# Summing modulation rows on VectorE and GpSimd before TensorE adds the partitions

## The chip, the cores and the metric

One core of one Trainium2 chip runs the whole program. The metric is device time in microseconds (us), the median over runs. Engines: TensorE (PE, with its weight loads as PEld), VectorE (DVE), ScalarE (ACT), GpSimd (POOL) and SyncE (SP), which only issues DMAs. All data are fp32.

## The reference, cut to what matters

Two transformer blocks run one after the other on 512 tokens of 1024 features. Each is steered by a modulation, a vector times a matrix:

```
mod   = silu(c)     @ w_ada    + b_ada       # block 1: (1, 3072): shift, scale, gate
mod   = silu(c_2)   @ w_ada_2  + b_ada_2     # block 2: (1, 6144): shift, scale, gate, shift2, scale2, gate2
mod_c = silu(c_ctx) @ w_ada_2  + b_ada_2     # block 2, for the context rows
```

Block 1: norm and modulate, projections of 3072 columns, a recurrent branch (convolution, gates, a scan) and a dilated attention, output projection, gated sum. Block 2: norm and modulate, projections, pooling, differential attention, an RWKV branch, gates, a merge and a mixture of 32 experts with two per token. The modulation is 9216 columns of a matrix with 1024 rows: 18 chunks of 512 columns. Chunks 0 to 3 (shift and scale of block 1) are needed at once; the change concerns chunks 4 to 17. Chunks 4 and 5 serve one vector (c), 6 to 9 two (c_2 and c_ctx), 10 to 17 only c_2.

## The kernel before, in words

The program is written by hand, engine by engine. Each stage has a function for each engine (`proj1_tensor`, `proj1_vector`, ...), and five program functions at the end call them in order; each engine runs its list in that order and waits on semaphores. VectorE, ScalarE and GpSimd also wait for their own last instruction before the next (`Line`, lines 90 to 210). All instructions of one kind therefore have one line in the profile (154 two tensors, 159 and 160 with scalars, 164 scalar and tensor, 168 copy, 172 reciprocal, 176 fill, 192 scan, 204 activation, 207 matmul, 210 transpose, 143 DMA).

Weights lie in DRAM as chunks of 128x4096, 2 MB each. SyncE streams them into three buffers in the order of `MAIN_CHUNKS` (line 323); a load waits until TensorE has used the chunk three places earlier (`load`). A chunk of the modulation holds its 1024 rows as 8 groups k of 128 partitions, with 512 columns each.

The stages up to the change's last step, in order:

- Preparation: modulation chunks 0 to 3, first norm.
- First projections (`proj1_*`): 24 steps t (chunks 6 to 11 of the stream, four tiles each) of 8 matmuls 128x128 by 512. The recurrent branch runs beside them (`lru_*`): VectorE convolves at steps 0 to 3, ScalarE and VectorE make its gates, VectorE scans at steps 4 to 7, ScalarE squares at step 8; at step 9 TensorE sums the squares. At steps 8 to 15 VectorE copies each tile (`raw1`) and TensorE turns it by a matmul one step later (`rotate`).
- Attention of block 1 (`att_*`): 35 steps x for 32 pairs of query block (128 to 512 keys) and head. In a step TensorE does the scores of x+1, transposes x-2 and multiplies x-3 with the values; VectorE adds a mask and takes the maximum; ScalarE does the exponential and copies the transposes. Four times, once per query block, ScalarE leaves for a square and a square root, with a table load on both sides.
- Output projection (`out1_*`): four row tiles of two matmul groups, then norms of six row tiles on VectorE and ScalarE (`normed`), each turned by TensorE (`turn8`).
- Projections of block 2 (`proj2_*`).

Modulation chunks 4 to 17 go through TensorE. `modulation_blocks` multiplies each 128x128 block of a chunk by the vectors, held as 32 columns of which three count; the 32 rows of result for each quarter t of the chunk go to partitions 32t to 32t+31, so one bank's 128 columns hold all 512:

```
for k in ks:
    for t in range(4):
        T.mm(b[32 * t:32 * t + 32, 0:128], cs[:, k, :], w[:, k, c4(t)], k == 0, k == 7)
```

A chunk is 32 such matmuls, and an fp32 matmul leaves two records in the trace. Chunks 4 to 15 are dealt out in thirds (`ADA`, `ADA_K`, line 863), one third to an attention step (`ada_tensor`); chunks 16 and 17 follow the output projection in `out1_tensor`. `ada_vector` adds the bias (kept as 128 partitions in the arena), `ada_gpsimd` stores the rows to `mods1` and `mods2` in DRAM, from where they are read back, broadcast to 128 partitions. GpSimd otherwise only issues DMAs and fills buffers in these stages.

## Time and profile before

| | us |
|---|---|
| median of 3 runs (lowest, highest) | 1869.82 (1866.83, 1871.75) |
| the profiled execution: span, which is the only time given for it | 1876.8 |
| TensorE busy in it | 1717.6 |
| VectorE, ScalarE, GpSimd busy | 804.7, 518.8, 109.4 |
| first projections, from the first matmul to the first scores | 36.9 to 221.9 |
| attention of block 1 | 221.9 to 309.6 |
| output projection, to the last quarter of the first tile of block 2 | 309.6 to 391.4 |

A row of the profile gives a line of the program, an engine, an operation, what it writes and reads (`arena` is the one SBUF tensor, `psum` the accumulators, `in_w` the chunks in DRAM), how often, the busy time, the mean duration, and the idle time in front of it with what ended it. TensorE's records overlap, so that busy times of groups of its rows can sum to more than the stretch. PEclk is the granted clock as a share of 2.4 GHz.

### The profile page before, as it was taken

How to read it: one execution, taken by the hardware profiler on the slowest of the kernel's cores; microseconds unless marked ns; L12 is line 12 of the kernel's file. 1: busy time of each engine (PE TensorE's matmuls, PEld its weight loads, DVE VectorE, ACT ScalarE, POOL GpSimd, SP SyncE). 2: the span in 40 equal slices, each digit the busy share in tenths (PEclk: the TensorE clock that was granted, in tenths of full speed). 3: DMA queues.
4: the chain of work that ended last, by engine and by line, in shares of the span. 5: the costliest groups of instructions: out<-in, count | busy, mean ns of one | idle time of the engine just before them, and what ended most of it. 6: DMA issues, size and time to landing. Idle time of an engine off the chain costs nothing.

```text
span 1876.8 us, 37887 instructions
## 1 busy us (share of the span) xinstructions
PE 1717.6 (92%) x16822; PEld 927.4 (49%) x16822; DVE 804.7 (43%) x1484; ACT 518.8 (28%) x983; POOL 109.4 (6%) x144
## 2 busy tenths in 40 slices
PE   5999999999999999999999999999999977778786
PEld 3444566544546555556667667544454333323332
DVE  3853144656627456355654554344462211222210
ACT  3710254311127422354453341122231110101010
POOL 0000010010000000100000000000001101010100
PEclk8999989999989999999998998899999999999998
DMA  9121376351110030042221210356569999999997
GB/s 396 76 88 47 145 287 247 145 224 69 45 45 1 23 151 0 17 170 82 77 81 50 63 56 24 114 219 221 219 239 398 416 425 415 422 413 425 417 423 279
DMA packets 48360, 359.25 MB, mean 191 GB/s; under 512 B 8325, under 2 KB 8557, under 8 KB 28736
## 3 DMA queue, kind: packets, MB, share of 16 engines
q1 hardware_dynamic: 35792, 311.51, 41.2%
q0 software_dynamic: 12400, 45.27, 7.3%
q8 instruction: 134, 2.20, 0.5%
q14 instruction: 34, 0.28, 0.0%
HBM read 337.47 MB, written 27.32 MB: 194 GB/s over the span
## 4 chain that ended last, share of the span: by engine, by line
PE 74%; DMA 16%; ACT 4%; issue 3%; DVE 2%; POOL 0%; SPq 0%; ACTq 0%; DVEq 0%; POOLq 0%
PE psum L207 71%; DMA arena<-in_w 16%; PE psum L210 3%; ACT arena L204 3%; ACT L204 1%; DVE arena L154 1%; DVE arena L180 0%; DVE arena L164 0%; DVE arena L172 0%; DVE arena L160 0%; POOL arena L141 0%; DMA arena<-in_tok 0%; DVE arena L168 0%; DVE arena L159 0%; POOL out L149 0%
## 5 line engine op out<-in xcount | busy, mean ns | idle before, releaser
L207 PE MATMUL psum<-arena 32*32 32x16 f32 (+12 forms) x16178 | 1638.1, 304 | 145.2 <-DMA arena<-in_w 73.4
L207 PEld LDWEIGHTS psum<-arena 32*32 32x32 f32 (+5 forms) x16178 | 856.0, 135 | 876.3 <-issue 764.7
L204 ACT ACTIVATE arena<-psum 128x512 f32<-128x512 f32 (+5 forms) x334 | 171.4, 513 | 871.2 <-PE psum L207 670.7
L154 DVE TENSOR_TENSOR arena<-arena,psum 128x512 f32<-128x512 f32 (+3 forms) x128 | 64.9, 507 | 402.6 <-PE psum L207 209.2
L154 DVE TENSOR_TENSOR arena<-arena 128x512 f32<-128x512 f32 (+10 forms) x315 | 191.6, 608 | 31.0 <-ACT arena L204 14.7
L204 ACT ACTIVATE arena<-arena 128x512 f32<-128x512 f32 (+10 forms) x254 | 138.8, 546 | 177.7 <-DVE arena L154 41.9
L204 ACT ACTIVATE arena<-psum,arena 128x128 f32<-128x128 f32 (+3 forms) x221 | 111.7, 505 | 275.1 <-PE psum L210 135.5
L154 DVE TENSOR_TENSOR arena<-psum,arena 128x128 f32<-128x128 f32 (+3 forms) x116 | 47.4, 409 | 154.5 <-PE psum L207 141.3
L164 DVE SCALAR_TENSOR_TENSOR arena<-arena 128x512 f32<-128x512 f32 (+7 forms) x162 | 103.5, 639 | 14.5 <-ACT arena L204 8.1
L210 PE MATMUL psum<-arena 128*128 128x128 f32 x644 | 102.6, 291 | 6.1 <-ACT arena L204 3.2
L172 DVE RECIPROCAL arena<-arena 128x1 f32<-128x1 f32 (+4 forms) x71 | 79.1, 1113 | 63.0 <-ACT arena L204 59.2
L210 PEld LDWEIGHTS psum<-arena 128*128 128x128 f32 x644 | 73.6, 146 | 64.3 <-issue 46.0
L164 DVE SCALAR_TENSOR_TENSOR arena<-psum,arena 128x512 f32<-128x512 f32 (+4 forms) x84 | 49.6, 591 | 114.8 <-PE psum L207 111.2
L204 ACT ACT_TABLE_LOAD x68 | 87.2, 1283 | 18.8 <-DMA arena<-gd 11.6
L159 DVE TENSOR_SCALAR arena<-arena 128x32 f32<-128x32 f32 (+10 forms) x126 | 39.8, 316 | 57.7 <-ACT arena L204 52.7
L184 DVE COPY_PREDICATED arena<-arena,psum 128x512 f32<-128x512 uint32 (+1 forms) x60 | 35.9, 598 | 45.4 <-PE psum L207 41.3
L168 DVE COPY arena<-psum 128x512 f32<-128x512 f32 (+4 forms) x53 | 27.8, 525 | 63.2 <-PE psum L210 35.4
L180 DVE TENSOR_REDUCE arena<-psum 128x1 f32<-128x768 f32 x32 | 30.6, 958 | 47.8 <-PE psum L207 46.0
L149 POOL DMA_INDIRECT out<-arena x16 | 25.1, 1566 | 408.6 <-DVE arena L164 139.5
L143 POOL DMA_DIRECT2D arena<-kd x28 | 21.1, 753 | 240.9 <-DVE arena L154 135.3
L143 POOL DMA_DIRECT2D mods<-arena x26 | 14.4, 557 | 312.4 <-DVE arena L154 304.2
L160 DVE TENSOR_SCALAR arena<-psum,arena 128x128 f32<-128x128 f32 x64 | 26.2, 410 | 8.5 <-PE psum L210 5.0
(49 smaller groups left out, 177.7 us busy)
## 6 DMA issues: line engine op xcount, KB each, us to landing
arena<-in_w SPq DMA_DIRECT2D x127, 2048.0 KB, 34.5
arena<-in_w SPq DMA_DIRECT2D x48, 256.0 KB, 3.1
arena<-in_w SPq DMA_DIRECT2D x12, 1024.0 KB, 36.4
arena<-kd POOLq DMA_DIRECT2D x28, 256.0 KB, 3.4
gd<-arena SPq DMA_DIRECT2D x24, 256.0 KB, 3.2
arena<-gd SPq DMA_DIRECT2D x24, 256.0 KB, 5.6
arena<-in_w POOLq DMA_DIRECT2D x2, 2048.0 KB, 9.6
kd<-arena POOLq DMA_DIRECT2D x2, 1536.0 KB, 11.0
```

What stands on the lines that cost most here:

```text
L143: self.e.dma_start(out, in_).then_inc(*signal)
L154: return self.ends(self.e.tensor_tensor(out, a, b, op))
L159: return self.ends(self.e.tensor_scalar(out, a, s1, None, op0))
L160: return self.ends(self.e.tensor_scalar(out, a, s1, s2, op0, op1))
L164: return self.ends(self.e.scalar_tensor_tensor(out=out, in0=a, scalar=s, in1=b, op0=op0, op1=op1))
L168: return self.ends(self.e.tensor_copy(out, a))
L172: return self.ends(self.e.reciprocal(out, a))
L180: return self.ends(self.e.tensor_reduce(out, a, AX, op, negate=negate))
L184: return self.ends(self.e.copy_predicated(out, mask, a))
L204: return self.ends(self.e.activation(out, a, func, **kw))
L207: return self.ends(self.e.matmul(out, lhs, rhs, start=start, stop=stop))
L210: return self.ends(self.e.transpose(out, a, ident))
```

## The change

VectorE and GpSimd now do the multiplication by the vector: for each chunk and vector, eight blocks of 128x512 are scaled by a per-partition number and summed, which leaves 128 partitions to add. TensorE does that with a column of ones (`one_column`): four matmuls for each sum. VectorE sums chunks 4 to 7 between the steps of the first projections (`ADA_ROWS`), from half chunks that SyncE loads into two buffers of their own; GpSimd sums chunks 8 to 17 from quarter chunks that it loads itself into two more, one multiplication and one addition per block, from the first projections on, with four buffers for its sums. The bias now goes into DRAM first and the rows are added to it by an accumulating DMA. These chunks leave the stream of weights; `ADA_SUMS` says at which step TensorE adds, `STORES` behind which quarter GpSimd stores. The diff, cut to its core:

```diff
+    def add(self, out, in_, signal):
+        self.e.dma_start(out, in_, accum_op=ALU.add).then_inc(*signal)
...
-YTBANK = (2,)
+YTBANK = (4,)
...
-MAIN_CHUNKS = [0, 1, 2, 3, 6, 7, 8, 9, 10, 11, 4, 5, *range(14, 24), 12, 13, 24, 25, *range(26, 34), *range(40, 45)]
+MAIN_CHUNKS = [0, 1, 2, 3, 6, 7, 8, 9, 10, 11, 12, 13, *range(26, 34), *range(40, 45)]
...
+            V.zero(cs[:, 0, 16:17], value=1.0)
...
         def proj1_sync():
-            for c in (6, 7, 8, 9, 10, 11):
+            for c in (6, 7, 8):
                 load(c)
+            half_load(0)
+            half_load(1)
+            load(9)
+            load(10)
+            half_load(2)
+            half_load(3)
+            load(11)
+            for n in (4, 5, 6, 7):
+                half_load(n)
...
                 lru_tensor(t)
+                if ("p1", t) in ADA_SUMS:
+                    ada_tensor(ADA_SUMS["p1", t], ALL8)
...
                 lru_vector(t)
+                if ("p1", t - 1) in ADA_SUMS:
+                    ada_vector(ADA_SUMS["p1", t - 1])
+                for n in range(*ADA_ROWS.get(t, (0,))):
+                    ada_rows_vector(n)
...
+        ADA = (4, 8, 5, 6, 9, 7, 10, 11, 12, 13, 14, 15, 16, 17)
+        BY_VECTOR = (4, 5, 6, 7)
+        ADA_VECTORS = {j: (0,) if j < 6 else (1, 2) if j < 10 else (1,) for j in ADA}
+        ADA_SUMS = {("p1", 11): 4, ("p1", 13): 8, ("p1", 16): 5, ("p1", 19): 6, ("p1", 20): 9, ("p1", 21): 7, ("p1", 22): 10,
+                    ("att", 0): 11, ("att", 4): 12, ("att", 18): 13, ("att", 30): 14, ("out1", 1): 15, ("out1", 3): 16, ("pool", 2): 17}
+        ADA_ROWS = {7: (0, 2), 8: (2, 4), 9: (4, 8), 10: (8, 10), 13: (10, 13), 14: (13, 16), 15: (16, 18), 16: (18, 21),
+                    17: (21, 24), 18: (24, 28), 19: (28, 32)}
+        BY_POOL = [(j, v) for j in range(8, 18) for v in ADA_VECTORS[j]]
...
+        def ada_rows_vector(n):
+
+            j, k = 4 + n // 8, n % 8
+            w = half_in[n // 4 % 2][:, k % 4, :]
+            if k % 4 == 0:
+                V.wait_ge(d_ah[n // 4 % 2]["half", n // 4])
+            for v in ADA_VECTORS[j]:
...
+                    V.ts(ada_sum(j, v), w, cs[:, k, v:v + 1], None, ALU.mult)
+                else:
+                    V.stt(ada_sum(j, v), w, cs[:, k, v:v + 1], ada_sum(j, v), ALU.mult, ALU.add)
...
+        def ada_rows_gpsimd(n):
+
+            j, q = 8 + n // 4, n % 4
+            G.wait_ge(d_ap[n % 2]["piece", n])
+            for v in ADA_VECTORS[j][::-1]:
+                s = BY_POOL.index((j, v))
+                if q == 0 and s > 3:
+                    G.wait_ge(T["ada", BY_POOL[s - 4][0]])
+                for k in range(2):
+                    w, by = piece_in[n % 2][:, k, :], cs[:, 2 * q + k, v:v + 1]
+                    if q == 0 and k == 0:
+                        G.ts(sums_g[s % 4], w, by, None, ALU.mult)
+                    else:
+                        t = w if v == 1 else sqj
+                        G.ts(t, w, by, None, ALU.mult)
+                        G.tt(sums_g[s % 4], sums_g[s % 4], t, ALU.add)
+            G.then_inc("piece", n)
...
+        def ada_tensor(j, ring):
+            T.wait_ge(V["half", 2 * j - 7] if j in BY_VECTOR else G["piece", 4 * j - 29], *ps.take(ring, "ada", j))
+            last = ADA_VECTORS[j][-1]
+            for v in ADA_VECTORS[j]:
+                for t in range(4):
+                    T.mm(ps["ada", j][32 * t:32 * t + 32, 0:128], one_column(v), ada_sum(j, v)[:, c4(t)],
+                         v == ADA_VECTORS[j][0], v == last)
+            T.then_inc("ada", j)
...
         def lru_gpsimd():
...
+            STORES = {9: (4,), 10: (8,), 14: (5,), 17: (6,), 18: (9,), 20: (7,), 22: (10,), 23: (11,), 25: (12,), 29: (13,), 33: (14,), 37: (15,)}
+            piece_load(0)
+            piece_load(1)
+            for n in range(40):
+                ada_rows_gpsimd(n)
+                if n + 2 < 40:
+                    piece_load(n + 2)
+                for j in STORES.get(n, ()):
+                    ada_gpsimd(j)
...
-                ada_tensor(*next(steps), MBANK)
+                if ("att", x) in ADA_SUMS:
+                    ada_tensor(ADA_SUMS["att", x], MBANK)
...
-            for step in steps:
-                ada_tensor(*step, MBANK)
...
-            for j in (16, 17):
-                for q in range(3):
-                    ada_tensor(j, q, ALL8)
```

## Rows read from the trace of the kernel before

**Rows 1.** The page, part 1: busy time, share of the span, instructions.
```profile
PE 1717.6 (92%) x16822; PEld 927.4 (49%) x16822; DVE 804.7 (43%) x1484; ACT 518.8 (28%) x983; POOL 109.4 (6%) x144
```

**Rows 2.** The page, part 4: the chain of waits by engine.
```profile
PE 74%; DMA 16%; ACT 4%; issue 3%; DVE 2%; POOL 0%; SPq 0%; ACTq 0%; DVEq 0%; POOLq 0%
```

**Rows 3.** Busy time by stretch: PE, PEld, DVE, ACT, POOL, clock, DMA share, GB/s.
```profile
57.00:106.50 49.50, 49.50 (x117) 22.00 (x116) 42.24 (x45) 32.87 (x38) 0.00 (x0) 1.00 0.20 69
...
168.00:221.90 53.90, 53.90 (x128) 23.59 (x126) 4.47 (x7) 5.46 (x8) 0.00 (x0) 1.00 0.18 70
221.90:309.60 87.70, 86.23 (x1009) 56.83 (x1009) 44.85 (x95) 46.99 (x112) 11.06 (x20) 0.94 0.74 280
```

**Rows 4.** Weight loads grouped by shape, attention (221 to 310 us): busy, mean ns, idle.
```profile
L207 PEld LDWEIGHTS psum<-arena 128*32 128x32 f32 x724 | 18.5, 113 | 6.1 <-issue 4.8
```

**Rows 5.** Timeline, attention: start, length, instruction, idle before it.
```profile
243.87 0.59 PEld L207 LDWEIGHTS psum<-arena 128*32 128x32 f32 x24 [0.17 <-issue]
244.66 0.88 PEld L207 LDWEIGHTS psum<-arena 128*128 128x128 f32 x6 [0.20 <-issue]
...
250.38 2.35 PE L207 MATMUL psum<-arena 128*128 128x64 f32 x6 [1.11 <-ACT arena L204]
```

**Rows 6.** Busy time by stretch of 2 us, attention; the clock is third from last.
```profile
250.00:252.00 2.00, 1.62 (x6) 1.09 (x6) 0.50 (x2) 1.72 (x5) 1.01 (x2) 0.69 0.93 213
252.00:254.00 2.00, 2.00 (x20) 0.96 (x22) 1.11 (x2) 0.63 (x4) 0.00 (x0) 0.50 0.99 426
```

**Rows 7.** VectorE's instructions grouped by shape, 57.0 to 106.6 us.
```profile
L164 DVE SCALAR_TENSOR_TENSOR arena<-arena 128x512 f32<-128x512 f32 x13 | 9.5, 733 | 0.5
L154 DVE TENSOR_TENSOR arena<-arena 128x512 f32<-128x512 f32 x12 | 8.3, 692 | 0.4
L192 DVE TENSOR_TENSOR_SCAN arena<-arena 128x512 f32<-128x512 f32 x4 | 4.9, 1224 | 0.1
...
L159 DVE TENSOR_SCALAR arena<-arena 128x512 f32<-128x512 f32 x4 | 1.7, 426 | 0.1
L160 DVE TENSOR_SCALAR arena<-arena 128x512 f32<-128x512 f32 x3 | 1.6, 547 | 3.7 <-ACT arena L204 3.6
```

**Rows 8.** Timeline of VectorE, first projections (steps 8, 9 and 20).
```profile
108.69 0.69 DVE L168 COPY arena<-psum 128x512 f32<-128x512 f32 x1 [2.20 <-PE psum L207]
...
116.41 0.69 DVE L154 TENSOR_TENSOR arena<-psum,arena 128x512 f32<-128x512 f32 x1 [6.31 <-PE psum L207]
...
202.01 0.69 DVE L154 TENSOR_TENSOR arena<-arena,psum 128x512 f32<-128x512 f32 x1 [26.68 <-ACT arena L204]
```

**Rows 9.** GpSimd's instructions grouped by shape, the whole span.
```profile
L143 POOL DMA_DIRECT2D mods<-arena x26 | 14.4, 557 | 312.4 <-DVE arena L154 304.2 <-DVE arena L172 8.2
L176 POOL MEMSET arena<- 128x1024 f32 x8 | 7.6, 952 | 130.1 <-ACT arena L204 129.7
...
L176 POOL MEMSET arena<- 128x256 f32 x2 | 0.6, 311 | 0.1
```

**Rows 10.** DMA issues: count, KB each, us to landing (issued at 37.1 us).
```profile
arena<-in_norm_att POOLq DMA_DIRECT2D x1, 256.0 KB, 12.9
```

**Rows 11.** Timeline, 784 to 800 us: GpSimd's fills and a scan of VectorE.
```profile
787.76 9.09 POOL L176 MEMSET arena<- 128x1024 f32 x12 [129.71 <-ACT arena L204]
...
790.85 1.23 DVE L192 TENSOR_TENSOR_SCAN arena<-arena 128x512 f32<-128x512 f32 x1
```

**Rows 12.** Timeline, end of the output projection.
```profile
373.75 3.70 PE L207 MATMUL psum<-arena 128*32 128x128 f32 x128
...
381.20 8.44 PE L207 MATMUL psum<-arena 128*128 128x384 f32 x16 [3.75 <-DMA arena<-in_w]
...
382.63 1.23 DVE L154 TENSOR_TENSOR arena<-arena 128x1024 f32<-128x1024 f32 x1
...
389.48 1.04 PE L210 MATMUL psum<-arena 128*128 128x128 f32 x8
```

**Rows 13.** Busy time by stretch of 10 us, output projection; the clock is third from last.
```profile
380.00:390.00 10.00, 8.80 (x21) 5.10 (x22) 3.26 (x5) 1.04 (x3) 3.06 (x5) 0.66 0.95 394
```

More of the change, by code:

```diff
@@ L414, in build @@
             dma(n) for n in ("par", "cst", "x", "bias", "lnc", "pos", "wbd", "na")]
-        d_mod = [dma(f"mod{i}") for i in range(3)]
+        d_mod = [dma(f"mod{i}") for i in range(5)]
         d_g1, d_n1, d_n3, d_tb, d_xd, d_br, d_rw, d_gn = [
@@ L450, in build @@
         XA, XC = ar.get(2064, m=4, s=516), ar.get(2048, m=4, s=512)
+        half_in = [r0[:, 2048 * i:2048 * i + 2048].rearrange("p (k n) -> p k n", k=4) for i in range(2)]
+        sums_v = [bsum[:, 512 * i:512 * i + 512] for i in range(3)] + [sq1[:, 512 * i:512 * i + 512] for i in range(2)]
+        piece_in = [A_[:, NCOL - 4096 + 1024 * i:NCOL - 3072 + 1024 * i].rearrange("p (k n) -> p k n", k=2) for i in range(2)]
+        sums_g = [A_[:, NCOL - 2048 + 512 * i:NCOL - 1536 + 512 * i] for i in range(4)]
         dead = Arena(A_, 0, ar.top)
@@ L463, in build @@
         Sb, Pb, PTb, YB = [*sl[0:2], Sb3], [sl[2], sl[3], Pb3], sl[4:6], sl[6:8]
+        arow = [ar.get(128) for _ in range(5)]
         YBT = XA.rearrange("p m s -> p (m s)")[:, 0:2048].rearrange("p (m s) -> p m s", m=4)
@@ new lines, in piece_load @@
+        def piece_load(n):
+            if n > 1:
+                G.wait_ge(G["piece", n - 2])
+            G.dma(piece_in[n % 2].rearrange("p k n -> p (k n)"), T_["w"][ada_chunk(8 + n // 4), :, 1024 * (n % 4):1024 * (n % 4) + 1024],
+                  d_ap[n % 2].up("piece", n))
+        def ada_rows_gpsimd(n):
[9 more added lines that the diff above has]
+                        G.ts(sums_g[s % 4], w, by, None, ALU.mult)
+                    else:
+                        t = w if v == 1 else sqj
+                        G.ts(t, w, by, None, ALU.mult)
+                        G.tt(sums_g[s % 4], sums_g[s % 4], t, ALU.add)
+            G.then_inc("piece", n)
@@ L882, in ada_vector @@
             ps.free(V.last(), "ada", j)
         def ada_gpsimd(j):
-            G.wait_ge(V["ada", j])
-            for v in ((0,) if j < 6 else (1, 2)):
+            p = ADA.index(j)
+            G.wait_ge(V["ada", j], d_bias["mods2"])
+            for v in ADA_VECTORS[j]:
                 dst = mods1[j * 512:(j + 1) * 512] if j < 6 else mods2[v - 1, (j - 6) * 512:(j - 5) * 512]
-                G.dma(dst.rearrange("(t n) -> t n", t=4), mrow[j % 3][v:128:32, :], d_mod[j % 3].up("mod", j))
+                G.add(dst.rearrange("(t n) -> t n", t=4), arow[p % 5][v:128:32, :], d_mod[p % 5].up("mod", j))
@@ L890, in mods_stored @@
         def mods_stored(j):
-            return [d_mod[i % 3]["mod", i] for i in range(max(4, j - 2), j + 1)]
-        def lru_sync():
-            for j in range(4, 16):
-                load(ada_chunk(j))
+            p = ADA.index(j)
+            return [d_mod[i % 5]["mod", ADA[i]] for i in range(max(0, p - 4), p + 1)]
         def lru_gpsimd():
             G.dma(nbb, T_["norm_att"].partition_broadcast(128), d_na.up("na"))
-            G.dma(bias, T_["bias"], d_bias.up("bias"))
-            for j in range(4, 16):
-                if j == 10:
+            G.dma(mods1, T_["bias1"], d_bias.up("mods1"))
@@ L1006, in scores @@
                 T.mm(ps["s1", x][:, 0:n], QT[hb:hb + 64, m, c4(i)], KT[hb:hb + 64, m, 0:n], True, True).then_inc("s1", x)
-            steps = iter(ADA)
             T.wait_ge(V["rope1", 9, 3], A["v1", 3])
@@ L1074, in att_vector @@
             for x in range(len(IT1) + 3):
-                if x % 3 == 0 and x:
-                    ada_vector(x // 3 + 3)
+                if ("att", x - 1) in ADA_SUMS:
+                    ada_vector(ADA_SUMS["att", x - 1])
                 if x < len(IT1):
@@ L1216, in out1_vector @@
                     normed(CX[:, i - 1, :], 3 + i, gsc, shc)
-            for j in (16, 17):
-                ada_vector(j)
+                if ("out1", i) in ADA_SUMS:
+                    ada_vector(ADA_SUMS["out1", i])
             turn8_dve("f2", 3, HT, 3)
@@ L1228, in build @@
                  [(n, m) for m in range(4) for n in ("kc", "k")] + [("v", m) for m in range(6)]
+        before = {b: a for a, b in zip([("start", 0)] + TILES2, TILES2)}
         CHUNK2 = {"pool": 26, "q": 27, "kc": 28, "k": 28, "v": 29}
@@ L1244, in proj2_gpsimd @@
             G.dma(xd, X.rearrange("p t d -> p (t d)"), d_xd.up("x"))
+            for j in (16, 17):
+                ada_gpsimd(j)
             G.wait_ge(V["b0", 3])
@@ L1363, in proj2_vector @@
                     late.step()
-                    continue
-                late.add(pooled(m) if n == "pool" else normed(n, m))
+                else:
+                    late.add(pooled(m) if n == "pool" else normed(n, m))
+                if before[n, m] in ADA_SUMS:
+                    ada_vector(ADA_SUMS[before[n, m]])
                 if (n, m) == ("pool", 3):
```

66 lines of the change are left out of this document (35 added, 31 removed).

## The prediction, made before the changed kernel ran

> **What bounds the kernel now.** The page's busy shares come first: TensorE is busy 92% of the span and no other engine half of it [rows 1]. The chain of waits agrees, with 74% of its length on TensorE and 16% on weight DMAs [rows 2]. Shares are averages, so the next view is the table by stretch, cut at stages that the change touches [rows 3]. In the first projections TensorE never pauses; in the attention stretch, 221.9 to 309.6, it is busy in all but 1.5 of 87.7 us, while ScalarE has 47.0 and VectorE 44.9; GpSimd's 11.1 are DMA issues alone. Before 392 us a microsecond taken from TensorE is therefore a microsecond of the end, unless another engine's chain is close behind. VectorE has 42.2 busy of 49.5 us between 57.0 and 106.5, then 4.5 of 53.9 from 168.0 on: full early, empty late.
>
> **Attention.** Twelve chunks leave this stretch. Their weight loads, 128 rows by 32 columns, are 18.5 us for 724 records [rows 4], 25.6 ns each; the program has 12 x 32 matmuls of two records, 768, so 19.6 us. The 6.1 us of idle in front of them is the change of operand at each of some 35 steps, which goes too: 25.7. Four sums (chunks 11 to 14) stay, 4 matmuls of two records each: 8 x 0.0256 + 0.37 (one change of operand in, 0.17, one out, 0.20 [rows 5]) = 0.58, four times 2.3. Net -23.4, and 64.3 us of TensorE remain. ScalarE's 47.0 with its gaps of about 0.1 us behind 112 instructions come to 58, so it is late next. Where it already was (1.11 us of wait at 250.38 [rows 5], behind two table loads), TensorE's granted clock then was 0.69 over 2 us and 0.50, the lower level of 1.2 GHz, over the next 2 [rows 6], and over three more such stretches; with 0.75 in the last the shortfall sums to 5.1 us, so such an episode costs 6.2. With less cover there will be more: between none and three (18.6). I take one, since the same detour of ScalarE comes once in each of four blocks and only one was exposed: **-17.2**.
>
> **First projections.** Seven sums are added: three of 8 records (4, 5, 10) and four of 16 (8, 6, 9, 7): 88 x 0.0256 + 7 x 0.37 = **+4.9**, on TensorE and so on the path. VectorE takes 48 new operations on 128x512: 42 at 0.733 us and 6 at 0.426 [rows 7], 33.3 us. Two of them (1.2 us) stand ahead of the copy for the first rotation, which was done at 109.4 where TensorE came to it at 115.5, one 0.86 us matmul before the row at 116.41 [rows 8]: covered. The last 28 of them, 20.5 us, fall where VectorE idled 26.7 us [rows 8]; TensorE asks for the last sum five steps later: covered. SyncE's queue now waits for VectorE's rows before the third and later half chunks, with the loads of 9, 10 and 11 behind; two steps of cover each, nothing; the DMA engines, busy 0.18 to 0.20 of these stretches [rows 3], have room for the loads that move here.
>
> **GpSimd.** It gets 96 multiplications and 84 additions of 128x512, 40 loads and 18 stores. No row has its arithmetic. Its fills are 0.952 us for 1024 columns and 0.311 for 256 [rows 9], hence 0.53 for 512: the lower end of any pass. For an addition, with two operands read, I take twice that, 1.05, as an estimate (upper end three times, 1.6). 96 x 0.53 + 84 x 1.05 = 139 us, plus 40 loads and 18 stores at 0.56 of issuing each [rows 9]: 171. Its first load goes out behind a queue whose loads took 12.9 us to land [rows 10], so it begins at about 51 us. Buffers tie it to TensorE: piece 8 needs sum 8 (step 13, about 150 us), piece 16 needs sum 9 (step 20, done at about 201, just before VectorE's row at 202.01 [rows 8]). From there the four pieces of chunk 12 take 14 us, ready at about 216 against the fourth attention step at about 230: TensorE waits for none.
>
> **Beside each other.** Whether the two engines slow each other no row shows for arithmetic. The nearest row is a scan on VectorE in the middle of GpSimd's fills: 1.23 us [rows 11], against 1.224 in the projections [rows 7], no difference. The ends are 0 and full turn-taking (21 us, the rival below). I take the nearest row's value, **0**, and keep the other for the range. The Trainium skill, "SBUF — State Buffer", section "Who interferes with whom", says that a VectorE instruction with two SBUF inputs contends with a GpSimd instruction that reads SBUF, not with one that only writes it, and that the later of the two is blocked for the whole instruction of the other. By that rule the trace agrees, since a fill reads nothing, and the sum would be the rival's. No other term rests on it.
>
> **Output projection.** Chunks 16 and 17 were 128 loads, 3.70 us at 373.75; then TensorE waited 3.75 for chunk 26 [rows 12], whose load is now queued right behind chunk 13 and is there long before. But TensorE's next need is VectorE's last normed row, ready at 383.86 (382.63 + 1.23 [rows 12]), and the turning could start then instead of at 389.48: at most -5.5. Against it stand sums 15 and 16, 1.15, and the clock: 0.66 over 380 to 390 us [rows 13] after the old wait; the new one is about as long, and what it slows are now the transposes and the last quarter of the pool projection, some 2.5. Sum **-1.9** (-6 to +1). Sum 17 in the pool projection: **+0.6**.
>
> **Sum.** -17.2 + 4.9 + 0 - 1.9 + 0.6 = -13.6 us. The profiled execution's span, 1876.8, is the only time given for it, 7.0 above the median of the three runs, 1869.8; everything counted is a difference early in a chain that TensorE carries on, so it comes off the median: 1856. About 0.3% (5.6 us) is what a measurement of this kernel can tell from no change.
>
> **Rival 1, the two engines take turns: slower.** The place is VectorE's chain from 57.0 to 106.5: 13 + 12 + 4 operations with two SBUF operands and 7 scalar ones [rows 7], 36 in all. If GpSimd has one of its own in hand each time, VectorE waits for it, 0.77 us on average (139 us over 180), 27.7. Take off 8% for GpSimd's issuing, 1.5 for the operations behind the four reciprocals, 5.5 of VectorE's idle time there: 18.5 us later. TensorE's cover at the first rotation is 115.5 - 109.4 - 1.2 = 4.9, so it waits 13.6; the clock behind the wait costs up to 5, and the rows of steps 13 and 16 to 19 some 2.5: 21. Net +7.4, 1877; with additions at 1.6 us about 1885, with a half-busy GpSimd 1866. It decides once VectorE is 5 us late, and turns the sign at a wait of 13.6. For it: nothing else here would slow a covered engine, and VectorE is 85% busy just there. Against it: the only overlapped row shows nothing. Chance 0.36.
>
> **Rival 2, attention shrinks less.** Three exposed detours with their clock instead of one: 12.4 less, net -1.2, 1869. For it: ScalarE and its gaps need 58 of the 64 us. Against: TensorE's order runs two to three heads apart, which covers 2 to 4 us. Chance 0.12.
>
> **Rival 3, GpSimd too slow for its sums.** TensorE stands in attention until a sum is ready. At three times my prices four pieces take 42 us from 202, so sum 12 is 14 late, and 13 and 14 about 5 more: net +5, 1875; beyond that 1890 and more. For it: no row has the arithmetic. Against: 14 us of cover at the tightest sum. Chance 0.08.
>
> **How the numbers follow.** The forecast has 0.44; its own range is 1845 (no exposed detour, the full 5.5) to 1864 (two detours). Faster by over 0.3%: 0.42 of it and 0.03 of rival 2, 0.45. Within 0.3%: 0.02 of the forecast, 0.08 of rival 2, 0.12 of rival 1: 0.22. Slower: 0.24 of rival 1, 0.08 of rival 3, 0.01 of rival 2: 0.33. The range goes from 1845 up to rival 1 with the dearer additions, 1886, leaving out its end and rival 3's.
>
> **What would show it.** Right: no 32-column weight loads of 16 to 24 a step in attention, that stretch near 70 us; scans and two-operand operations of VectorE at 1.22 and 0.69 to 0.74 us before 106 us; the copy at step 8 before 112 us; no wait for in_w at 381. Rival 1: the same operations longer, or with gaps of half a microsecond in front of each, GpSimd's too, and TensorE idle 10 us and more at about 116 us, released by VectorE. Rival 2: waits for ScalarE in attention with the clock at 0.5 behind them. Rival 3: waits for GpSimd in front of the sums. The forecast is wrong if the first projections end later than 230 us or attention takes over 80.

## The result, and the profile after

The changed kernel took 1915.0 us (median of 4 runs, 1908.6 to 1925.4) against 1870.8 for the kernel before on the same chip: a ratio of 1.0254, 95% interval 1.0224 to 1.0285. It is slower by 2.5%; 1856 had been forecast, with a range up to 1886. The ratios, here and below, leave out executions more than 1.5% above the fastest of their kernel; the medians hold all. The profiled execution has a span of 1912.7 us, 35.9 more than that of before; the medians are 44.2 apart, largely since the profile of before is a long execution (its span is above all four times of that kernel, 1866.8 to 1875.4). The marks below compare the two profiles, so they account for the 35.9.

First part 1 and part 4 of the page of the changed kernel, the lines that answer to [rows 1] and [rows 2]:

```profile
PE 1737.5 (91%) x16070; PEld 935.5 (49%) x16070; DVE 876.0 (46%) x1533; ACT 518.5 (27%) x983; POOL 410.7 (21%) x357
...
PE 61%; DMA 18%; POOL 10%; ACT 4%; DVE 4%; issue 3%; SPq 1%; ACTq 0%; POOLq 0%; DVEq 0%
```

TensorE has 752 instructions fewer than before and yet 19.9 us more of busy time (1737.5 against 1717.6): its work runs slower somewhere. And GpSimd, which was on 0% of the chain, is on 10% of it.

TensorE's timeline in the changed kernel (start, length, instruction, idle before it and what ended it) shows where the end moved:

```profile
121.30 2.93 PE L210 MATMUL psum<-arena 128*128 128x512 f32 x3 [5.12 <-DVE arena L171]
...
237.54 0.48 PE L213 MATMUL psum<-arena 128*128 128x128 f32 x1 [0.76 <-ACT arena L207]
...
257.98 2.00 PE L210 MATMUL psum<-arena 128*32 128x128 f32 x12 [16.48 <-POOL arena L157]
...
311.25 3.38 PE L210 MATMUL psum<-arena 128*128 128x64 f32 x8
...
373.72 7.39 PE L210 MATMUL psum<-arena 128*128 128x512 f32 x24
...
428.57 31.63 PE L210 MATMUL psum<-arena 128*128 128x128 f32 x88 [0.88 <-DVE arena L171]
```

The same points in the kernel before:

```profile
224.71 0.33 PE L210 MATMUL psum<-arena 128*128 128x128 f32 x1
...
283.41 1.83 PE L207 MATMUL psum<-arena 128*128 128x64 f32 x8
...
334.95 7.03 PE L207 MATMUL psum<-arena 128*128 128x512 f32 x16
...
391.39 61.27 PE L207 MATMUL psum<-arena 128*128 128x128 f32 x162 [0.88 <-DVE arena L168]
```

Three points of the program serve as marks below, in every run: the first transpose of attention (here 237.54, before 224.71), the second half of the second row tile of the output projection (here 373.72, before 334.95; "the output mark" below) and the last quarter of the first tile of block 2 (here 428.57, before 391.39; "the last mark"). So of 37.2 us up to the last mark the first projections bring 12.8, the stretch from attention to the output mark 25.9 (136.2 in place of 110.2), and the rest gives 1.6 back. After the last mark the changed kernel's execution is the shorter by 1.3 us.

Within the 25.9 the largest single row is the wait of 16.48 us for GpSimd's sum of chunk 12. The table by stretch of the changed kernel (PE, PEld, DVE, ACT, POOL, clock, DMA share, GB/s) shows the remainder:

```profile
237.00:239.00 2.00, 1.46 (x4) 0.86 (x4) 1.57 (x6) 1.20 (x5) 1.90 (x2) 0.59 0.87 332
...
240.00:260.00 20.00, 3.52 (x18) 2.17 (x18) 1.10 (x4) 1.52 (x7) 18.43 (x17) 0.50 0.20 58
260.00:280.00 20.00, 19.73 (x60) 12.85 (x60) 10.43 (x25) 11.84 (x34) 18.17 (x16) 0.50 0.27 78
...
300.00:320.00 20.00, 20.00 (x61) 12.75 (x60) 7.66 (x14) 9.37 (x20) 18.04 (x16) 0.50 0.26 76
...
340.00:360.00 20.00, 20.00 (x88) 13.72 (x88) 6.09 (x10) 5.62 (x11) 18.14 (x15) 0.75 0.28 80
```

The granted clock is 0.50, the level of 1.2 GHz, during the wait and for nearly all of attention behind it, where TensorE is hardly waiting for anything: it is busy 20.00 of 20 us at 300, while VectorE has 7.7 and ScalarE 9.4. Before, attention had 0.94 [rows 3]. The first row shows that the clock fell at 237 to 239 us, before the long wait, which begins at 241.5. The row at 311.25 holds eight records, two of a score product of 64x512 and six of value products of 128x64; they take 3.38 us, and a group of the same make took 1.83 before (at 283.41, granted 1.00).

GpSimd's instructions in the changed kernel, first from 30 to 480 us, then from 262 to 340 us, where VectorE has little to do (busy us, mean ns):

```profile
L162 POOL TENSOR_SCALAR arena<-arena 128x512 f32<-128x512 f32 x96 | 166.9, 1738 | 29.6 <-DMA arena<-in_w 22.9 <-POOL arena L157 0.2
L157 POOL TENSOR_TENSOR arena<-arena 128x512 f32<-128x512 f32 x84 | 111.7, 1330 | 7.0
...
L162 POOL TENSOR_SCALAR arena<-arena 128x512 f32<-128x512 f32 x22 | 37.0, 1681 | 1.3
L157 POOL TENSOR_TENSOR arena<-arena 128x512 f32<-128x512 f32 x20 | 25.5, 1276 | 1.7
```

A product costs 1.7 us, an addition 1.3: 278.6 us of arithmetic where I had counted 139. And VectorE's instructions from 57 to 140 us, which answer to [rows 7]:

```profile
L167 DVE SCALAR_TENSOR_TENSOR arena<-arena 128x512 f32<-128x512 f32 x21 | 22.1, 1053 | 0.8
L157 DVE TENSOR_TENSOR arena<-arena 128x512 f32<-128x512 f32 x17 | 17.6, 1034 | 0.6
L175 DVE RECIPROCAL arena<-arena 128x512 f32<-128x512 f32 x4 | 13.4, 3353 | 0.1
L195 DVE TENSOR_TENSOR_SCAN arena<-arena 128x512 f32<-128x512 f32 x4 | 6.6, 1646 | 0.1
L162 DVE TENSOR_SCALAR arena<-arena 128x512 f32<-128x512 f32 x6 | 4.4, 734 | 0.4
L157 DVE TENSOR_TENSOR arena<-arena,psum 128x512 f32<-128x512 f32 x4 | 2.8, 688 | 2.3 <-ACT arena L207 1.9
```

The instructions with two SBUF operands are longer by a third and more on average (1053 against 733 ns, 1034 against 692, 1646 against 1224), with hardly a gap in front of them, and so is the operation with a scalar, which reads one SBUF operand (734 against 426); the reciprocal with one operand (3353, before 3354) and the operation with one operand in PSUM (688, before 686) are not. The copy at step 8 starts at 120.56 in place of 108.69 [rows 8], and TensorE's wait of 5.12 us stands at 121.30.

### The profile page after: what moved, and what is told of

It reads as the page before. It is cut to its first block, busy times and chain, and to the rows that moved or that the text cites. A ratio compares the mean times of both kernels' runs of the same rounds, so it can differ in the third digit from the quotient of the medians.

```text
span 1912.7 us, 36645 instructions
## 1 busy us (share of the span) xinstructions
PE 1737.5 (91%) x16070; PEld 935.5 (49%) x16070; DVE 876.0 (46%) x1533; ACT 518.5 (27%) x983; POOL 410.7 (21%) x357
## 4 chain that ended last, share of the span: by engine, by line
PE 61%; DMA 18%; POOL 10%; ACT 4%; DVE 4%; issue 3%; SPq 1%; ACTq 0%; POOLq 0%; DVEq 0%
PE psum L210 57%; DMA arena<-in_w 18%; POOL arena L162 5%; PE psum L213 4%; POOL arena L157 3%; ACT arena L207 3%; DVE arena L157 1%; ACT L207 1%; DVE arena L167 1%; POOL arena L143 1%; SPq L143 1%; POOL mods L146 0%; DVE arena L171 0%; DVE arena L183 0%; DVE arena L163 0%
## 5 line engine op out<-in xcount | busy, mean ns | idle before, releaser
L210 PE MATMUL psum<-arena 32*32 32x16 f32 (+9 forms) x15426 | 1650.0, 309 | 156.6 <-DMA arena<-in_w 59.5
L210 PEld LDWEIGHTS psum<-arena 32*32 32x32 f32 (+4 forms) x15426 | 859.3, 138 | 888.6 <-issue 760.1
L157 DVE TENSOR_TENSOR arena<-arena 128x512 f32<-128x512 f32 (+10 forms) x315 | 203.4, 646 | 31.6 <-ACT arena L207 15.2
L162 POOL TENSOR_SCALAR arena<-arena 128x512 f32<-128x512 f32 x96 | 166.9, 1738 | 29.6 <-DMA arena<-in_w 22.9
L167 DVE SCALAR_TENSOR_TENSOR arena<-arena 128x512 f32<-128x512 f32 (+7 forms) x204 | 154.5, 757 | 15.9 <-ACT arena L207 7.7
L213 PE MATMUL psum<-arena 128*128 128x128 f32 x644 | 112.6, 311 | 10.7 <-DVE arena L157 6.5
L213 PEld LDWEIGHTS psum<-arena 128*128 128x128 f32 x644 | 79.7, 156 | 79.9 <-issue 54.4
L157 POOL TENSOR_TENSOR arena<-arena 128x512 f32<-128x512 f32 x84 | 111.7, 1330 | 7.0
L162 DVE TENSOR_SCALAR arena<-arena 128x512 f32<-128x512 f32 (+8 forms) x132 | 45.6, 345 | 58.1 <-ACT arena L207 53.0
L171 DVE COPY arena<-psum 128x512 f32<-128x512 f32 (+4 forms) x67 | 31.9, 476 | 76.5 <-PE psum L210 46.1
L187 DVE COPY_PREDICATED arena<-arena,psum 128x512 f32<-128x512 uint32 (+1 forms) x60 | 35.9, 598 | 44.5 <-PE psum L210 40.0
```

The lines of the kernel that those rows point to most:

```text
L157: return self.ends(self.e.tensor_tensor(out, a, b, op))
L162: return self.ends(self.e.tensor_scalar(out, a, s1, None, op0))
L167: return self.ends(self.e.scalar_tensor_tensor(out=out, in0=a, scalar=s, in1=b, op0=op0, op1=op1))
L171: return self.ends(self.e.tensor_copy(out, a))
L187: return self.ends(self.e.copy_predicated(out, mask, a))
L210: return self.ends(self.e.matmul(out, lhs, rhs, start=start, stop=stop))
```

## The experiments

Three causes are in the trace at once: the wait for sum 12, the longer VectorE instructions, and the half clock. The half clock could be a consequence of the wait or stand by itself. The first four runs separate these. Ratios are to the kernel before, run beside each.

### The sums taken up later

```diff
-("att", 0): 11, ("att", 4): 12, ("att", 18): 13, ("att", 30): 14, ("out1", 1): 15, ("out1", 3): 16, ("pool", 2): 17
+("att", 6): 11, ("att", 22): 12, ("att", 31): 13, ("out1", 0): 14, ("out1", 2): 15, ("pool", 1): 16, ("q", 1): 17
```

> TensorE takes up the sums of chunks 11 to 17 later (attention steps 6, 22 and 31, output projection steps 0 and 2, second-projection tiles pool 1 and q 1), when GpSimd has long finished them; GpSimd's own work is unchanged. Theory 'the wait': the 16.5 us wait for sum 12 at attention step 4 is the loss, and it also sets the clock back; without it attention is granted 1.00, takes 70 to 75 us instead of 114, and the time is 1868 to 1880 us. Theory 'thin attention': without the 128x32 matmuls of the loads TensorE's granted clock falls in attention with or without a wait; the clock reads 0.50 between 240 and 320 us again, only the 16.5 us go, and the time is 1896 to 1902 us.

Measured: 1910.2 us, ratio 1.0202 (1.0165 to 1.0240). The wait for GpSimd is gone, the half clock is not. Table by stretch, TensorE's timeline, and VectorE's two-operand instructions on 1024 elements in the output projection (335 to 440 us):

```profile
240.00:260.00 20.00, 20.00 (x67) 12.98 (x66) 10.14 (x25) 10.65 (x30) 18.69 (x17) 0.50 0.29 91
300.00:320.00 20.00, 20.00 (x59) 12.19 (x58) 8.58 (x14) 9.94 (x20) 18.04 (x16) 0.50 0.19 58
...
362.81 8.82 PE L210 MATMUL psum<-arena 128*128 128x512 f32 x16 [6.37 <-DVE arena L171]
...
L157 DVE TENSOR_TENSOR arena<-arena 128x1024 f32<-128x1024 f32 x11 | 18.9, 1716 | 0.4
```

Theory "the wait" falls as a theory of the clock. Even the 16.5 us came back only in part: the stretch takes 120.1 us net of its last wait (126.5 between the marks, less 6.37), and the output projection now waits 6.37 us for a copy on VectorE, which is still at its norms there; these two-operand instructions take 1716 ns beside GpSimd, against 1.23 us before [rows 12].

### The kernel before, with three quarters of the loads' matmuls left out

Rows 128 to 895 of each chunk are left out of the modulation; no arithmetic on GpSimd.

```diff
-        ADA_K = (range(3), range(3, 6), range(6, 8))
+        ADA_K = (range(0, 1), range(0), range(7, 8))
```

> The kernel before, with only rows 0 to 127 and 896 to 1023 of chunks 4 to 17 multiplied (8 of 32 TensorE matmuls of each chunk; the other six eighths of these modulation rows are left out); loads, waits and engines as before, no GpSimd arithmetic. Theory 'the wait': attention loses three quarters of the 23.4 us that I had counted, the output projection 2.8 us: 1848 to 1853 us, granted clock 0.9 to 1.0 in attention. Theory 'thin attention': the granted clock falls to 0.50 in attention although nothing new is waited for; attention takes 85 to 110 us, and the time is 1865 to 1890 us.

Measured: 1891.2 us, ratio 1.0119 (1.0086 to 1.0152): less work than before, and slower. Table by stretch, and TensorE's timeline at the output mark:

```profile
260.00:280.00 20.00, 20.00 (x77) 11.59 (x75) 8.42 (x16) 8.29 (x18) 3.35 (x6) 0.50 0.57 197
...
357.89 7.03 PE L207 MATMUL psum<-arena 128*128 128x512 f32 x16
```

The first transpose is at 224.85, so the stretch takes 133.0 us in place of 110.2. TensorE waits once, 1.5 us for ScalarE right at its start; the kernel before waits 1.1 us at 250 us and has the clock back some 10 us later [rows 5, 6]. Taking matmuls out of attention is enough to keep it on the lower clock.

### The changed kernel without GpSimd's arithmetic

GpSimd forms one product per vector and chunk and touches one element of every other quarter, and its sums of chunks 8 to 17 are left out; loads, waits and stores stay.

```diff
-                for k in range(2):
+                for k in range(1 if q == 0 else 0):
...
+            if q:
+                G.ts(piece_in[n % 2][:, 0, 0:1], piece_in[n % 2][:, 0, 0:1], cs[:, q, 1:2], None, ALU.mult)
```

> The changed kernel with GpSimd's arithmetic left out but for one product per vector and chunk (and one element per piece): the sums of chunks 8 to 17 are not formed, their loads, waits and stores stay. Theory 'the wait': no wait for sum 12, VectorE's two-operand instructions back at 690 to 735 ns, first projections 8 to 11 us shorter, attention about 70 us at a granted clock of 1.00: 1850 to 1862 us. Theory 'thin attention': wait and lengthening go, 25 to 28 us, but attention stays at 0.50 for most of its length: 1880 to 1892 us.

Measured: 1884.6 us, ratio 1.0087 (1.0054 to 1.0119). VectorE's instructions from 57 to 140 us, the table by stretch, and two marks of TensorE's timeline:

```profile
L167 DVE SCALAR_TENSOR_TENSOR arena<-arena 128x512 f32<-128x512 f32 x22 | 16.6, 757 | 0.8
L157 DVE TENSOR_TENSOR arena<-arena 128x512 f32<-128x512 f32 x18 | 12.4, 691 | 0.6
L195 DVE TENSOR_TENSOR_SCAN arena<-arena 128x512 f32<-128x512 f32 x4 | 4.9, 1224 | 0.1
...
260.00:280.00 20.00, 20.00 (x64) 12.20 (x64) 10.11 (x20) 10.18 (x22) 5.78 (x9) 0.50 0.22 68
...
227.16 0.33 PE L213 MATMUL psum<-arena 128*128 128x128 f32 x1 [0.76 <-ACT arena L207]
...
346.09 7.39 PE L210 MATMUL psum<-arena 128*128 128x512 f32 x24
```

VectorE's instructions are back at their old length, and attention's first transpose is at 227.16 in place of 237.54: GpSimd's arithmetic cost the first projections some 10.4 us (1.0 of it is a later start of the profiled execution, 38.04 against 37.07). Its whole price is 30.4 us (1915.0 - 1884.6). What is left of the change is still 13.6 us slower than before (1884.64 - 1871.05), with attention at 0.50 and no wait over 1.1 us in it; the stretch takes 118.9 us.

### Filler in attention

```diff
+                if x > 4 and all(("att", y) not in ADA_SUMS for y in (x, x - 1, x - 2)):
...
+                    for n in range(24):
+                        T.mm(PSUM[32 * (n % 4):32 * (n % 4) + 32, 7, 128:256], cs[:, n // 4, :], ident, True, True)
```

> The changed kernel with 24 more 128x32 matmuls of constants (their results are never read) in 22 of the 35 attention steps; the wait for sum 12 stays. Theory 'the wait': more work for TensorE is only slower: 22 x 24 x 0.06 us = 30 us at full clock, 1940 to 1975 us. Theory 'thin attention': the work brings the clock back to 1.00 within the attention, its steps go from 3.0 us towards the 2.4 to 3.0 us of the kernel before, and the time falls to 1888 to 1908 us in spite of more work.

Measured: 1919.4 us, ratio 1.0261 (1.0232 to 1.0291). Table by stretch, and a group of the same make as the one at 311.25 above:

```profile
260.00:280.00 20.00, 20.00 (x275) 14.29 (x275) 6.20 (x13) 4.96 (x18) 18.17 (x16) 0.71 0.26 80
280.00:300.00 20.00, 20.00 (x345) 14.71 (x346) 9.37 (x20) 11.27 (x28) 18.39 (x15) 1.00 0.26 81
...
321.74 1.83 PE L210 MATMUL psum<-arena 128*128 128x64 f32 x8
```

The clock is back at 1.00 from 280 us on, and the group takes 1.83 us in place of 3.38. Of the two halves of the expectation the clock came true and the time did not: 24 matmuls are twice what the kernel before had in a step, and they use up what the clock gives (121.3 us between the marks net of the 16.5 us wait, against 119.7 in the changed kernel). Still, some 500 additional matmuls cost 4 us in all, where at the full clock I had put 30.

### Half of the loads' matmuls

The kernel before with rows 256 to 767 left out.

```diff
-        ADA_K = (range(3), range(3, 6), range(6, 8))
+        ADA_K = (range(0, 1), range(1, 2), range(6, 8))
```

> The kernel before, with 16 of the 32 TensorE matmuls of each of chunks 4 to 17 (rows 256 to 767 left out of these modulation rows). If half of the 128x32 work still holds the clock in attention: granted 0.9 to 1.0 there, 11 to 12 us less than before in attention and 1.8 in the output projection, 1855 to 1860 us. If it does not: granted 0.50 from the first attention steps on, as with a quarter of the work (1891 us), and a little longer than that, 1890 to 1902 us.

Measured: 1904.9 us, ratio 1.0187 (1.0130 to 1.0245); granted 0.50 from 240 to 340 us, 153.3 us between the marks. A quarter of the matmuls at half clock 133.0, half of them 153.3, all of them at nearly the full clock 110.2: as long as the clock stays low, more matmuls only make the stretch longer.

### Six chunks on VectorE, none on GpSimd

A first attempt at a version that keeps the clock: chunks 4, 5 and 14 to 17 are summed by VectorE in its idle time, 6 to 13 stay TensorE loads, spread over 32 attention steps.

```diff
-        BY_VECTOR = (4, 5, 6, 7)
+        BY_VECTOR = (4, 5, 16, 17, 14, 15)
+        BY_TENSOR = (6, 7, 8, 9, 10, 11, 12, 13)
...
+                for part in [next(steps, None)]:
+                    if part:
+                        ada_part(*part)
```

> VectorE sums chunks 4, 5, 14, 15, 16 and 17 (one vector each) in its idle time from projection step 9 on; chunks 6 to 13 stay TensorE loads, 8 matmuls in each of 32 attention steps in place of 12; GpSimd does no arithmetic. If 8 matmuls a step hold the clock: attention 7 to 8 us shorter than before, the output projection and the wait for the pool weights 5 to 7 us shorter, six sums 2 to 3 us in the first projections: 1856 to 1864 us, faster than before. If they do not: granted 0.50 in attention, 125 to 135 us of it, 1885 to 1905 us.

Measured: 1909.2 us, ratio 1.0168 (1.0113 to 1.0223). Table by stretch:

```profile
240.00:260.00 20.00, 18.46 (x183) 11.04 (x181) 9.27 (x21) 11.37 (x29) 3.38 (x4) 0.86 0.69 255
260.00:280.00 20.00, 20.00 (x117) 11.93 (x110) 8.12 (x15) 6.66 (x15) 0.84 (x1) 0.50 0.38 145
```

Attention starts at the full clock here, loses it at TensorE's wait of 1.5 us for ScalarE at 253 us, and does not get it back before 340. The kernel before has nearly the same wait (1.11 us [rows 5]) and recovers. The profiled execution took 1914.1 us; the mean clock of all six, 1885.2 to 1915.8 us, is 0.938 to 0.956, where the kernel before beside them has 0.956 to 0.971.

### GpSimd starts behind VectorE's chain

```diff
             piece_load(1)
+            G.wait_ge(V["ya", 3])
             for n in range(40):
```

(`ADA_SUMS`, `STORES` and the order of `ADA` moved back to suit.)

> As the changed kernel with later sums, but GpSimd's arithmetic starts only when VectorE has finished its chain of scans in the first projections (about 108 us, in place of 57.7), and the sums of chunks 8 to 17 are moved back accordingly. Theory 'contention in VectorE's chain': the first projections end at 225 to 228 us as before the change, not at 235; attention at 0.50 as in the other runs; 1884 to 1896 us. Rival 'GpSimd's work costs the same wherever it lies': VectorE's instructions are lengthened later instead (rotary tables, attention softmax), first projections or attention 8 to 12 us longer by that; 1900 to 1912 us.

Measured: 1942.5 us, ratio 1.0391 (1.0345 to 1.0437). The first transpose of attention is at 228.58, 9.0 us earlier than in the changed kernel: the first projections get most of their time back when GpSimd starts later, as the theory says (0.8 of it is an earlier start, 37.21 against 38.04, and two of the seven sums there now come later). But the total is the worst of all. TensorE's waits from 225 to 480 us (in total, times, longest), and one row of VectorE's timeline:

```profile
PE psum L210 <- DVE arena L157: 29.0, 2, 28.1
PE psum L210 <- POOL arena L157: 13.6, 2, 8.6
...
459.21 1.42 DVE L157 TENSOR_TENSOR arena<-arena 128x512 f32<-128x512 f32 x2 [31.59 <-DMA arena<-in_ropes]
```

GpSimd's arithmetic now ends so late that its sums are waited for twice in attention (13.6 us) and that the load of the rotary tables, which stands behind it on GpSimd's queue, comes 28 us late for the second projections. Both waits are of my making; neither theory had them.

### GpSimd multiplies by a constant

```diff
-                    w, by = piece_in[n % 2][:, k, :], cs[:, 2 * q + k, v:v + 1]
+                    w, by = piece_in[n % 2][:, k, :], 0.5
```

> The changed kernel with GpSimd multiplying by the constant 0.5 in place of the modulation vector's column (these rows of the modulation are wrong by that): measures what a product of a chunk row by a scalar held per partition costs more than one by a constant. If the per-partition scalar is what makes GpSimd's product 1.56 us: products of 0.5 to 0.6 us, GpSimd 90 to 100 us less busy, no wait for sum 12 (time 1885 to 1898 us). If the operation itself costs that: 1.5 to 1.75 us again, the same wait of 16 us, 1910 to 1918 us.

Measured: 1907.7 us, a single execution, with a wait of 14.5 us for sum 12. GpSimd's products from 262 to 340 us:

```profile
L162 POOL TENSOR_SCALAR arena<-arena 128x512 f32<-128x512 f32 x22 | 35.6, 1617 | 1.1
```

1617 ns against 1681: the scalar's place is not the price, the operation is.

### Two and four chunks on VectorE

To keep the twelve matmuls of each attention step, only the output projection's chunks leave TensorE (16 and 17), or these and 14 and 15.

```diff
-        BY_VECTOR = (4, 5, 6, 7)
+        BY_VECTOR = (16, 17)
+        BY_TENSOR = (4, 5, 6, 7, 8, 9, 10, 11, 12, 13, 14, 15)
```

> Only chunks 16 and 17 leave TensorE: VectorE sums them in its idle time between projection steps 13 and 16 (16 instructions, 12 us), TensorE adds the partitions at steps 16 and 18; chunks 4 to 15 are TensorE loads in attention with 12 matmuls a step as before the change, GpSimd does no arithmetic. If the dense 128x32 work is what holds the clock in attention: granted 0.9 to 1.0 there, attention as long as before; the output projection ends 3.7 us of matmuls and most of a 3.75 us wait earlier: 1862 to 1868 us, faster than before by 0.1 to 0.5%. If the gain is eaten by VectorE's chain behind the output projection: 1868 to 1872 us.

> As the run with two, and chunks 14 and 15 on VectorE too: ten chunks are TensorE loads in attention, 12 matmuls a step in the first 30 of 35 steps, none after. If the clock is held while the 12 matmuls last and the last five steps are too few to matter: attention 3 to 4 us shorter than before, 1857 to 1864 us. If the last steps lose the clock: 4 to 8 us longer than the run with two, 1868 to 1876 us.

Measured: two chunks 1878.6 us (twelve executions), ratio 1.0038 (1.0015 to 1.0060); four chunks 1896.0 us (nine executions), ratio 1.0057 (1.0025 to 1.0090). The profiled execution of the run with two shows what I had expected, attention as long as before (110.2 us between the marks) and the last mark at 388.09, 3.3 us earlier; but executions of this one kernel lay between 1868.6 us at a mean clock of 0.968 and 1909.8 at 0.940, of the one with four between 1878.7 and 1919.6, so the single profile must not be read for the median. In the profile of the run with four, attention dips as before, behind the same wait (1.10 us), and stays down for some 50 us:

```profile
260.00:280.00 20.00, 20.00 (x126) 12.12 (x123) 7.13 (x14) 6.06 (x15) 2.83 (x4) 0.50 0.43 159
...
300.00:320.00 20.00, 19.64 (x201) 13.14 (x201) 9.81 (x17) 9.50 (x18) 0.82 (x1) 0.91 0.43 161
```

Both expectations of a gain failed. In the run with four the clock stayed down although attention had the same twelve matmuls a step as before, so twelve a step do not ensure its return. Where the longer executions of the run with two lost their time no trace shows; that their mean clock is lower, with the same loads in attention as before, is open.

### Later sums and twelve filler matmuls a step

```diff
+                for n in range(12):
+                    T.mm(PSUM[32 * (n % 4):32 * (n % 4) + 32, 7, 128:256], cs[:, n // 4, :], ident, True, True)
                 if ("att", x) in ADA_SUMS:
```

> The changed kernel with later sums (no wait for sum 12) and 12 more 128x32 matmuls of constants in each of the 35 attention steps, as many as the kernel before had there for its loads; their results are never read. Theory 'thin attention': the clock is granted 0.9 to 1.0 in attention, which takes as long as before the change instead of at half clock, so this kernel is faster than the one with later sums alone (1910 us) by 12 to 25 us: 1885 to 1898 us; what is left above the kernel before is the lengthened first projections. If the clock falls for another reason (GpSimd's traffic, fewer loads in flight), it stays at 0.50 and the filler adds 25 to 50 us: 1930 to 1960 us.

Measured: 1905.0 us, ratio 1.0192 (1.0166 to 1.0217). Table by stretch:

```profile
240.00:260.00 20.00, 20.00 (x298) 13.51 (x289) 9.39 (x22) 8.90 (x27) 18.38 (x17) 1.00 0.27 83
260.00:280.00 20.00, 18.90 (x170) 11.63 (x170) 7.28 (x14) 8.04 (x21) 18.61 (x16) 0.74 0.27 80
280.00:300.00 20.00, 19.79 (x249) 13.00 (x248) 12.57 (x20) 11.32 (x24) 17.99 (x16) 1.00 0.27 81
```

With the same GpSimd traffic beside it, attention is granted 1.00 with one dip, as in the kernel before. That excludes GpSimd's traffic and the missing DMA loads as what keeps the clock low: matmuls of constants alone bring it back. The gain over later sums alone is 5.2 us, not 12 to 25: the stretch takes 113.1 us net of its last wait, against 120.1, so the filler eats most of what the clock gives.

### The loads of 16 and 17 behind the pool projection

The runs had shown one place where TensorE's matmuls are free: the wait for VectorE's last norm, 3.8 us behind the first pool projection. So the kernel before, with attention untouched, does its last 128 loads there.

```diff
+            load(26)
             load(24)
             load(25)
...
-            for j in (16, 17):
-                for q in range(3):
-                    ada_tensor(j, q, ALL8)
             T.wait_ge(W.landed(26), A["f2", 2, 0], V["f2", 2, 1], *ps.take(ALL8, "p2", "pool", 0))
...
+            for j in (16, 17):
+                for q in range(3):
+                    ada_tensor(j, q, ALL8)
             T.wait_ge(V["h2", 3])
```

(Chunks 24 and 25 take the buffers of 12 and 13, and 27 and 28 follow them.)

> The kernel before with the TensorE loads of chunks 16 and 17 moved behind the first pool projection (the pool weights are loaded ahead of them into the buffer that is free first); attention and every instruction elsewhere stay. In the run with two chunks on VectorE TensorE waited 3.8 us for VectorE's normalisation just there, and the second projections began 3.3 us earlier, at 388.1 us. If the 3.7 us of matmuls fit into that wait: the second projections begin at 388 to 389 us, 1866 to 1869 us, faster by 0.1 to 0.2%. If a load of the later weights (chunks 27 and 28 now wait for buffers freed some 10 us later) comes late: a new wait of 2 to 6 us behind the pool tiles, 1868 to 1875 us.

Measured: 1867.1 us against 1871.6, ratio 0.9978 (0.9957 to 0.9998). TensorE's timeline, which answers to [rows 5] and [rows 12], and the table by stretch:

```profile
247.46 1.50 PE L207 MATMUL psum<-arena 128*128 128x64 f32 x6 [1.10 <-ACT arena L204]
...
367.17 9.03 PE L207 MATMUL psum<-arena 128*128 128x384 f32 x144 [0.88 <-ACT arena L204]
376.37 1.09 PE L210 MATMUL psum<-arena 128*128 128x128 f32 x8 [0.17 <-DVE arena L154]
378.34 8.89 PE L207 MATMUL psum<-arena 128*128 128x128 f32 x32 [0.87 <-DVE arena L168]
389.07 52.62 PE L207 MATMUL psum<-arena 128*128 128x512 f32 x130 [1.84 <-DMA arena<-in_pool_w]
...
240.00:260.00 20.00, 18.90 (x220) 11.91 (x219) 10.89 (x24) 11.89 (x29) 4.41 (x8) 1.00 0.77 276
```

The row at 367.17 now holds both the pool projection and the 128 loads, the wait for chunk 26 is gone, and VectorE's norm is waited for 0.17 us: from the output mark to the last mark 50.9 us (378.34 - 327.42) in place of 56.4. Part of it is given back in a new wait of 1.84 us for the pool's own weights. This is the one version that beats both kernels, by 0.2%, at the edge of what can be told.

The same profile says something about the kernel before, whose attention is unchanged here: behind the same wait (1.10 us at 247.46) the clock stayed at 1.00, and the stretch took 105.6 us (327.42 - 221.81) in place of 110.2. So the dip of [rows 6] comes in some executions and not in others, and costs 4.6 us; the 7.5 us by which the output mark is earlier here is no work of this edit.

## Why the prediction was wrong

**Attention: the step that failed.** I took TensorE's 23.4 us of loads off and added "one exposed ScalarE detour", -17.2 in all. Net of the wait for sum 12 the stretch became 9.5 us longer (119.7 against 110.2; against an execution of the same attention without its dip, 105.6, it is 14.1), so this term was off by 26.7 us, and it turned the sign: without GpSimd's arithmetic the change should have brought 13.6 us, and it cost 13.6. I had the right symptom in hand, 0.50 over two microseconds behind a wait of 1.11 us [rows 5, 6], and priced it as an episode that ends by itself. The runs show that the loads had a part in its end: with all of them the clock came back after 10 us, with a half or a quarter of them, or four sums, it stayed at 1.2 GHz for nearly all of attention, and the filler restored it. What starts and ends an episode in a single execution stays open: once there was none behind the same wait, and once, with twelve matmuls a step, it lasted some 50 us. Half-clock work on TensorE takes longer than ScalarE's 58 us, so TensorE stayed the bound, busy 20.00 of 20 us. Rival 2 named this place, but with three episodes of 6.2 us, ending at 1869; its size was as wrong as the forecast's.

**First projections.** The seven sums themselves were forecast at +4.9 (88 x 0.0256 + 7 x 0.37 is 4.8); without GpSimd's arithmetic the first transpose moved by 2.4 (227.16 - 224.71). But the profile of before is late there: in the last experiment, whose first projections are those of before, this transpose is at 221.81 (clock 1.00 from 40 to 60 us, against 0.94), and against that the sums and the short waits behind them cost 5.4, near the forecast. VectorE's own 48 operations cost nothing visible, as forecast.

**Beside each other.** I took 0 between 0 and 21, from a scan beside GpSimd's fills [rows 11], and gave the turn-taking rival 0.36. It was some 10 us: rival 1 happened at half its price. A fill reads no SBUF, so that row was the nearest and could not show it. The Trainium skill, "SBUF — State Buffer", section "Who interferes with whom", has the right instructions: those with two SBUF operands lengthened, and so did the operation with a scalar, which it also names; the reciprocal and those with an operand in PSUM did not. That the one blocked waits for the whole instruction of the other the trace does not bear out as a rule for each pair: at 72.87 us a two-operand instruction of VectorE took its old 0.69 us, though by the trace a GpSimd product ran from 71.61 to 73.17, and on average these instructions lost 0.32 to 0.42 us beside GpSimd instructions of 1.3 to 1.7 us. The loss also reached the norms of the output projection (1.72 us for 1.23), which no rival had.

**GpSimd's prices.** 0.53 us for a product was a fill's price and the lower end of my bounds; the shortest took 1.56 us (one of them at 68.59, beside VectorE's reciprocal), the mean is 1.74. Additions, taken at 1.05 with an upper end of 1.6, took 1.33. Sum 12 was ready at 258 in place of 216, and rival 3, to which I gave 0.08 with "14 late", came true with 16.5. The bound from both sides was there for additions and missing for products. The Trainium skill, "GPSIMD Engine Reference", section 4.1, calls one-input operations on this engine "roughly line-rate", next to two-input ones that are about twice as slow as VectorE's; here the product with one input cost more than the addition with two.

**Output projection.** Forecast -1.9 for the stretch between the last two marks; measured -1.6. The wait for chunk 26 is gone, VectorE's last norm is the next thing late, waited for 3.8 us: right in place and size.

**Together.** 12.8 in the first projections (1.1 of it from a later start), 16.5 of wait, 9.5 net in attention at half clock, -1.6: 37.2 us between the profiles. In the prediction's own sums the forecast's range comes to 1846 to 1862 by its terms, where it says 1845 to 1864; nothing hangs on that. None of the three rivals was the outcome alone; their conditions were not exclusive, and I summed chances as if only one could come true.

## What to carry to other kernels

Before work is moved off an engine that is busy, leave it out in a trial: the kernel before without three quarters of these matmuls was 1.2% slower, and that one run contradicts the whole plan. A stretch of small matmuls that depend on other engines at each step may owe its clock to the bulk work between them; read the granted clock behind the smallest waits, and ask what is left to bring it back. Price an operation on an engine by a row with the same operands; where there is none, let the range go up as well as down, and look for what else stands on that engine's queue.

## What the runs showed of the hardware that had not been expected

- TensorE can be busy for the whole of a stretch by the profile and be granted 0.50 all through it: 20.00 of 20 us at 300 to 320 us in the changed kernel. Two records of a 64x512 product and six of 128x64 products take 3.38 us there and 1.83 at 1.00.
- A product of 128x512 fp32 by a scalar on GpSimd takes 1.56 to 1.74 us, with a constant hardly less (1.62 for 1.68), an addition of two such operands 1.27 to 1.33.
- Contention between GpSimd and VectorE appears as longer instructions, not as gaps between them: 0.73 us became 1.05 on average and a scan's 1.22 became 1.65.
- Executions of one and the same program can spread together with the granted clock: with two chunks moved off TensorE elsewhere, twelve spread over 41 us (mean clock 0.968 to 0.940), where 19 of the kernel before, run beside them, spread over 18 (0.970 to 0.959).
- Behind the same wait of 1.1 us for ScalarE, with the same attention, the clock fell to 0.50 for 10 us in one execution and stayed at 1.00 in another; the first took 4.6 us longer.
